# A three-block transformer layer on one core: statistics placed later, a split first unit, and a last product with tokens as rows

## The reference, cut to what matters

```python
x = x + 0.5 * swiglu_ffn(rmsnorm(x, ffn1_norm), ...)       # D_FF 2816
x = x + hybrid_mixer(rmsnorm(x, mix_norm), w_in, ...)      # sparse attention + gated linear attention
x = x + 0.5 * swiglu_ffn(rmsnorm(x, ffn2_norm), ...)
x = rmsnorm(x, final_norm)
# second layer
h = rms_norm(x, norm_pre_g);  proj = h @ w_in_2
y_a = pooled branch (window means, mix, silu(z_a));  y_b = mLSTM branch
merged = sigmoid(g_a + b0) * (y_a @ w_proj_pool) + sigmoid(g_b + b1) * (y_b @ w_proj_mlstm)
out = merged @ w_out_2
return x + rms_norm(out, norm_post_g)
```

## Time and profile before

| | us |
|---|---|
| median of 3 runs | 1795.54 |
| lowest, highest | 1794.02, 1796.08 |
| the profiled execution's own time | 1797.42 |
| its span, first to last instruction | 1795.6 |
| PE busy | 1693.2 (94% of the span) |
| PEld, weight loads beside matmuls | 1384.5 (77%) |
| DVE busy | 700.0 (39%) |
| ACT busy | 623.7 (35%) |
| POOL busy | 656.1 (37%) |

### The profile page before, as it was taken

One profiled execution on the slowest core, in us unless ns is written; L12 is line 12 of the kernel. 1 busy time (PEld: TensorE's weight loads), 2 busy tenths in 40 slices (PEclk: granted clock), 3 DMA queues, 4 the chain that ended last, 5 costly groups with the idle time before them and its releaser, 6 DMA issues.

```text
span 1795.6 us, 22547 instructions
## 1 busy us (share of the span) xinstructions
PE 1693.2 (94%) x7996; PEld 1384.5 (77%) x7996; DVE 700.0 (39%) x1157; ACT 623.7 (35%) x917; POOL 656.1 (37%) x281
## 2 busy tenths in 40 slices
PE   6999999999999999999999988889898999999997
PEld 5888888778886678888888877677677778877876
DVE  4333330225326744333330127473736331463223
ACT  4332231234236653223321234334343423234431
POOL 2444444433330024444444434222222223444443
PEclk9999999999999999999999989899999999999998
DMA  3322232233220002222222222121111112322221
GB/s 145 103 95 93 94 103 95 94 140 94 82 82 25 2 33 85 94 97 101 93 93 96 103 71 71 59 71 59 58 58 58 58 59 82 117 93 88 100 94 70
DMA packets 41663, 148.68 MB, mean 83 GB/s; under 512 B 4624, under 2 KB 4752, under 8 KB 41360
## 3 DMA queue, kind: packets, MB, share of 16 engines
q1 hardware_dynamic: 40112, 142.36, 23.4%
q10 hardware_dynamic: 1504, 5.66, 1.0%
HBM read 144.86 MB, written 2.10 MB: 82 GB/s over the span
## 4 chain that ended last, share of the span: by engine, by line
PE 47%; issue 39%; POOL 9%; DVE 3%; ACT 1%; POOLq 0%; DVEq 0%; ACTq 0%
PE ps L486 10%; PE ps L488 10%; PE ps L487 10%; POOL w_lo L432 9%; PE ps L566 3%; PE ps L568 3%; PE ps L567 3%; PE ps L724 1%; PE ps L494 1%; PE ps L736 1%; PE ps L746 1%; PE ps L501 1%; DVE scr L1518 1%; PE ps L647 0%; DVE scr L2068 0%
## 5 line engine op out<-in xcount | busy, mean ns | idle before, releaser
L432 POOL TENSOR_TENSOR w_lo<-w_raw,w_hi 128x1024 fp32r<-128x1024 f32 x262 | 636.1, 2428 | 1001.9 <-ACT w_hi L1067 992.4
L486 PE MATMUL ps<-h_hi,w_hi 128*128 128x512 f32 x1504 | 600.6, 399 | 25.7 <-POOL w_lo L432 20.7
L1067 ACT ACTIVATE w_hi<-w_raw 128x1024 fp32r<-128x1024 f32 x260 | 275.5, 1060 | 945.5 <-PE ps L488 763.5
L487 PE MATMUL ps<-h_lo,w_hi 128*128 128x512 f32 x1504 | 592.0, 394 | 0.0
L488 PE MATMUL ps<-h_hi,w_lo 128*128 128x512 f32 x1504 | 591.6, 393 | 0.0
L486 PEld LDWEIGHTS ps<-h_hi,w_hi 128*128 128x128 f32 x1504 | 287.2, 191 | 90.8 <-issue 22.1
L488 PEld LDWEIGHTS ps<-h_hi,w_lo 128*128 128x128 f32 x1504 | 286.3, 190 | 61.1
L487 PEld LDWEIGHTS ps<-h_lo,w_hi 128*128 128x128 f32 x1504 | 286.8, 191 | 58.9
L566 PE MATMUL ps<-hid_hi,w_hi 128*128 (+1 forms) x352 | 137.2, 390 | 1.8 <-POOL w_lo L432 1.8
L567 PE MATMUL ps<-hid_lo,w_hi 128*128 (+1 forms) x352 | 136.9, 389 | 0.0
L568 PE MATMUL ps<-hid_hi,w_lo 128*128 (+1 forms) x352 | 136.9, 389 | 0.0
(11 more groups left out here) (291 smaller groups left out, 1653.0 us busy)
## 6 DMA issues: line engine op xcount, KB each, us to landing
w_raw<-in_units SPq DMA_DIRECT2D x262, 512.0 KB, 3.2
x<-in_x SPq DMA_DIRECT2D x4, 512.0 KB, 7.1
w<-in_w ACTq DMA_DIRECT2D x1, 2048.0 KB, 8.1
out<-x SPq DMA_DIRECT2D x8, 256.0 KB, 2.0
scr<-proj ACTq DMA_DIRECT2D x8, 128.0 KB, 2.4
inv_count<-in_inv_count ACTq DMA_DIRECT2D x1, 1024.0 KB, 5.1
const<-in_const SPq DMA_DIRECT2D x1, 770.0 KB, 10.3
q_sc<-in_row_const ACTq DMA_DIRECT2D x1, 512.0 KB, 3.6
```

The costliest lines, as they stand in the source:

```text
L432: nc.gpsimd.tensor_tensor(w_lo[:, slot, :], w_raw[:, slot, :], w_hi[:, slot, :].bitcast(F32), ALU.subtract).then_inc(w_lo_done, 1)
L486: nc.tensor.matmul(ps[:, bank, :], whi, hi[:, k, :], start=(n == 0), stop=False)
L487: nc.tensor.matmul(ps[:, bank, :], whi, lo[:, k, :], start=False, stop=False)
L1067: nc.scalar.activation(w_hi[:, slot, :], w_raw[:, slot, :], ACT.Copy).then_inc(w_hi_done, 1)
```

## The change

1. **Later statistics.** Column sums stand behind the second unit, the spreading behind the third, in all three places. On ACT the heads and roots are put in the matching order; in `project` the copies that follow (`duplicate`) come one unit later.
2. **First unit split.** `first_unit` issues the two products with `w_hi` for all eight chunks and the eight with `w_lo` last, so `w_lo` is waited for after sixteen matmuls.
3. **Smaller first loads.** ACT first loads 8 columns of `param`, and the rest of `param` and `const` between the first heads. A one-element copy makes ACT load its table early. DVE starts when the gain is in.
4. **End of the first half of a feed-forward block.** DVE makes its four additions to `x` first, then four `raw_tail`; ACT converts the next unit's weights before the squares.
5. **x turned round.** In the pooled branch PE transposes `x` chunk by chunk (32 transposes in eight groups of four), ACT copies each group back. ACT also loads `g_row`, the last gain as a row on every partition (512 KB).
6. **Last product with tokens as rows.** Tokens of `m_hi` and `m_lo` are the stationary side, 512 columns of weights the moving one, with the eight chunks of `merged` as the outer loop and all eight banks filled at once. Per group of 128 tokens: ACT squares two banks with the sum accumulated, and takes the root; DVE the reciprocal, then two multiplications; POOL adds to six pieces, DVE to two; SP stores pieces of 128 tokens x 512 features. The 20 sums and 4 spreads at the end are gone.

```diff
-POOL_ADDS = 5
+POOL_ADDS = 6
...
+        PIECES = [(tt, half) for tt in range(TT) for half in range(2)]
+
+        def x_piece(n):
+            tt, half = PIECES[n]
+            return x[:, 4 * half:4 * half + 4, tt * P:(tt + 1) * P]
+
+        def sum_piece(n):
+            return scr[:, n, :].rearrange("p (c t) -> p c t", c=4)
...
+            for n, (tt, half) in enumerate(PIECES):
+                if n < POOL_ADDS:
+                    sp.wait_ge(x_out_pool, n + 1)
                 else:
-                    sp.wait_ge(x_out, c - POOL_ADDS + 1)
-                sp.dma_start(out[c * P:(c + 1) * P, :], x[:, c, :]).then_inc(out_sem, 16)
-            sp.wait_ge(out_sem, 16 * DC)
+                    sp.wait_ge(x_out, n - POOL_ADDS + 1)
+                sp.dma_start(out[tt * P:(tt + 1) * P, half * T:(half + 1) * T], scr[:, n, :]).then_inc(out_sem, 16)
...
+            for n in range(POOL_ADDS):
+                pool.wait_ge(sum_done, n + 1)
+                nc.gpsimd.tensor_tensor(sum_piece(n), sum_piece(n), x_piece(n), ALU.add).then_inc(x_out_pool, 1)
...
+            def first_unit(bank, chunks):
+                pe.wait_ge(w_hi_done, 1)
+                for k in range(DC):
+                    pe.wait_ge(*chunks(k))
+                    whi = w_hi[:, 0, k * P:(k + 1) * P]
+                    nc.tensor.matmul(ps[:, bank, :], whi, h_hi[:, k, :], start=(k == 0), stop=False)
+                    nc.tensor.matmul(ps[:, bank, :], whi, h_lo[:, k, :], start=False, stop=False)
+                pe.wait_ge(w_lo_done, 1)
+                for k in range(DC):
+                    mm = nc.tensor.matmul(ps[:, bank, :], w_lo[:, 0, k * P:(k + 1) * P], h_hi[:, k, :], start=False,
+                                          stop=(k == DC - 1))
                 mm.then_inc(unit_done, 1)
...
+                            opening = first and f == m == 0
+                            if opening and norm_of == 0:
+                                first_unit(4, raw(0))
+                            else:
+                                tile_unit(unit(u0 + 2 * f + m, 4, i), 4 + 2 * f + m, h_hi, h_lo,
+                                          raw(norm_of) if opening else None)
+                            if first and (f, m) == (0, 1):
+                                column_sums(norm_of)
+                            elif first and (f, m) == (1, 0):
+                                row_of_roots(norm_of)
...
                     tile_unit(unit(U_PROJ + u), project_bank(u), h_hi, h_lo, raw(1) if u == 0 else None)
-                    if u == 0:
+                    if u == 1:
                         column_sums(1)
-                    elif u == 1:
+                    elif u == 2:
                         row_of_roots(1)
...
-                with pe.Fori(0, DC) as i:
+                for j in range(DC):
+                    pe.wait_ge(ev_done, EV_POOL + j + 1)
+                    tile_unit(unit(U_POOL + j), 2 + j % 2, h_hi, h_lo)
+                    if j == 1:
+                        pe.wait_ge(mg_done, DC + 2)
+                    if j >= 4:
+                        pe.wait_ge(xt_done, j - 3)
+                    for tt in range(TT):
+                        mm = nc.tensor.transpose(ps[:, 4 + j % 4, tt * P:(tt + 1) * P], x[:, j, tt * P:(tt + 1) * P], ident)
+                    mm.then_inc(xt_ready, 1)
+                with pe.Fori(DC // 2, DC) as i:
                     for j in range(2):
                         pe.wait_ge(ev_done, EV_POOL + 2 * i + j + 1)
                         tile_unit(unit(U_POOL + j, 2, i), 2 + j, h_hi, h_lo)
+                pe.wait_ge(xt_done, DC)
...
-                pe.wait_ge(mg_done, 2 * DC + 2)
-                def two(i, chunks=None):
-                    for j in range(2):
-                        pe.wait_ge(out_done, 2 * i + j + 1)
-                        tile_unit(unit(U_OUT + j, 2, i), 2 + j, m_hi, m_lo, chunks if j == 0 else None)
-
-                two(0, lambda k: (m_lo_done, k + 1))
-                with pe.Fori(1, DC // 2) as i:
-                    two(i)
-                norm(5, "first")
-
-            pe.wait_ge(param_in, 16)
-            pe.wait_ge(small_in, 16)
+                for k in range(DC):
+                    u, _, slot = unit(U_OUT + k)
+                    pe.wait_ge(w_lo_done, u + 1)
+                    pe.wait_ge(m_lo_done, k + 1)
+                    for tt in range(TT):
+                        if k == 0 and tt >= 2:
+                            pe.wait_ge(mg_done, 2 * DC + tt - 1)
+                        tok = slice(tt * P, (tt + 1) * P)
+                        for half in range(2):
+                            acc, at = ps[:, 2 * tt + half, :], slice(half * T, (half + 1) * T)
+                            nc.tensor.matmul(acc, m_hi[:, k, tok], w_hi[:, slot, at], start=(k == 0), stop=False)
+                            nc.tensor.matmul(acc, m_lo[:, k, tok], w_hi[:, slot, at], start=False, stop=False)
+                            mm = nc.tensor.matmul(acc, m_hi[:, k, tok], w_lo[:, slot, at], start=False, stop=(k == DC - 1))
+                        if k == DC - 1:
+                            mm.then_inc(out_done, 1)
+                    if k < DC - 1:
+                        mm.then_inc(unit_done, 1)
...
                     for f in range(2):
-                        head(unit(u0 + 2 * f + 2, 4, i))
+                        if not (first and f):
+                            head(unit(u0 + 2 * f + 2, 4, i))
                         if first and f == 0:
+                            head(unit(u0 + 3))
                             root(norm_of)
+                            head(unit(u0 + 4))
                             root_row(norm_of)
-                            head(unit(u0 + 2 * f + 3, 4, i))
                         act.wait_ge(scaled_done, FT * n + 2 * i + f + 1)
...
                 streams(0, 4)
+                head(unit(ud + kps + 2))
                 squares(norm_of + 1, 0, 4)
-                head(unit(ud + kps + 2))
...
                     head(unit(U_PROJ + u + 2))
-                    if u == 0:
+                    if u == 1:
                         root(1)
-                    elif u == 1:
+                    elif u == 2:
                         root_row(1)
...
+                    act.wait_ge(xt_ready, j + 1)
+                    nc.scalar.activation(x[:, j, :], ps[:, 4 + j % 4, :], ACT.Copy).then_inc(xt_done, 1)
...
+                        act.dma_start(g_row[:, :], dram["g_post_row"]).then_inc(g_row_in, 16)
...
+                for i in range(DC - 2):
+                    head(unit(U_OUT + i + 2))
+                load_root()
+                for tt in range(TT):
+                    act.wait_ge(out_done, tt + 1)
+                    nc.scalar.activation(merged[:, 2 * (tt % 2):2 * (tt % 2) + 2, :], ps[:, 2 * tt:2 * tt + 2, :], ACT.Square,
+                                         accum_out=g_col[:, tt:tt + 1]).then_inc(osq_done, 1)
+                    act.wait_ge(osq_done, tt + 1)
+                    nc.scalar.activation(r_col[:, tt:tt + 1], g_col[:, tt:tt + 1], ACT.Sqrt, scale=1.0 / D, bias=c_("eps")
+                                         ).then_inc(orms_done, 1)
...
-            act.dma_start(param[:, :], dram["param"]).then_inc(param_in, 16)
-            act.dma_start(const[:, 0:FIRST_CONST], dram["const"][:, 0:FIRST_CONST]).then_inc(small_in, 16)
-            act.wait_ge(param_in, 16)
+            act.dma_start(param[:, 0:DC], dram["param"][:, 0:DC]).then_inc(gain_in, 16)
+            act.wait_ge(spare_done, 1)
+            nc.scalar.activation(spare[:, :], spare[:, :], ACT.Copy)
+            act.wait_ge(gain_in, 16)
...
+                    if c == 2:
+                        act.dma_start(const[:, 0:FIRST_CONST], dram["const"][:, 0:FIRST_CONST]).then_inc(small_in, 16)
+                    else:
+                        act.dma_start(param[:, DC:], dram["param"][:, DC:]).then_inc(param_in, 16)
...
-                        if gain is not None and d % 4:
+                        if gain is not None and d > 4:
                             raw_tail(next_norm, d - 1, gain)
                     if gain is not None:
-                        raw_tail(next_norm, 4 * half + 3, gain)
+                        for c in range(0 if half == 0 else DC - 1, 4 * half + 4):
+                            raw_tail(next_norm, c, gain)
...
+                dve.wait_ge(g_row_in, 16)
+                dve.wait_ge(xt_done, DC)
+                for n, (tt, half) in enumerate(PIECES):
+                    if half == 0:
+                        dve.wait_ge(orms_done, tt + 1)
+                        chain.link(nc.vector.reciprocal(r_col[:, tt:tt + 1], r_col[:, tt:tt + 1]))
+                    nc.vector.scalar_tensor_tensor(scr[:, n, :], ps[:, n, :], r_col[:, tt:tt + 1], g_row[:, half * T:(half + 1) * T],
                                                    ALU.mult, ALU.mult).then_inc(sum_done, 1)
-                for c in range(POOL_ADDS, DC):
-                    add(c)
-
```

(10 more changed lines are left out.)

59 lines of the change are left out of this document (21 added, 38 removed).

## The result

The changed kernel takes 1778.34 us (median of 4 runs, 1777.70 to 1782.81) beside 1795.17 us of the kernel before: a ratio of 0.991 (0.9895 to 0.9929), some 17 us less. Forecast were 1770.3 and a range of 1765.5 to 1776.5. The time lies 1.8 us above the range and 8.0 us above the forecast.

The account below looks back on a forecast made before the run. PE was taken as the bound, busy 94% of the span, limited by its 128 x 512 matmuls. Terms -8.0 - 1.8 - 5.9 - 2.3 + 3.0 - 1.7 - 8.5 = -25.2 from 1795.54 gave 1770.3, range 1765.5 to 1776.5.

Parts of the forecast that it names:

- Opening: Kernel start: PE starts earlier and sums no longer hold it; fourth unit starts at 31.8 instead of 39.8, 8.0 us earlier.
- the first rival: At the kernel's start `h_lo` stays the bound, PE runs longer at the lower clock: 5.2 instead of 8.0, 1773; chance 0.17.
- First block's middle: First feed-forward block, at 335.69: PE's wait for a `w_lo` goes, as ACT's squares now stand behind its `w_hi`: -1.8 us.
- projections: Column sums before the projections' spreading: the wait and slow clock behind it go, covered by the second unit: -5.9 us.
- Second feed-forward block: Column sums of the second feed-forward block: the wait goes as in the projections, less a new `w_lo` wait: -2.3 us.
- the small wait that was to appear under the old one: Second feed-forward block: the second unit's `w_lo` is ready only at 700.50, 0.6 us behind.
- Pooled branch: Eight groups of four transposes add 4.0 us on PE, a `w_lo` wait of 1.04 goes: +3.0 us net.
- Last product: Start of the last product: PE's wait of 1.71 us goes, since each `m_lo` chunk is needed only by its unit: -1.7 us.
- Tail: After the last matmul: the span ends 10.6 us later instead of 19.1, -8.5 us (7 to 10).
- the stages that the change leaves alone: Unedited stages: their waits and lower-clock stretches need not come out alike when everything shifts, 2 us either way.
- The lower clock that I had as a rival: Pooled branch: the clock falls behind each of eight transpose groups, nine matmuls at 0.43: +15 us, 1785; chance 0.03.
- Slower weight loads: Last product: activations loaded anew per matmul no longer run beside the matmuls: 36.7 us added, 1807; chance 0.02.

Follow-up runs that it names:

- early transposes: Changed kernel with the transposes of x moved from pooled branch to waits in the mLSTM's first head: 1776.2 us; with 64 small matmuls also split, 1771.3 us.

## Why the prediction was wrong, point by point

- **Opening: right, slightly too high.** TensorE starts at 7.13 and reaches the fourth unit at 32.42 (forecast 31.8, before 39.8): 7.4 instead of 8.0. Timelines of TensorE and VectorE in the changed kernel:

```profile
14.19 0.79 PE L509 MATMUL ps<-h_hi,w_hi 128*128 128x512 f32 x1 [1.18 <-DVE h_lo L1577]
...
16.92 2.99 PE L513 MATMUL ps<-h_hi,w_lo 128*128 128x512 f32 x8
...
25.22 0.95 PE L520 MATMUL ps<-const,scr 128*128 128x1 f32 x8
...
31.61 1.05 PE L527 MATMUL ps<-const,r_col 128*128 128x128 f32 x8
```

```profile
8.07 7.39 DVE L1577 SCALAR_TENSOR_TENSOR h_lo<-x,param,h_hi 128x512 fp32r<-128x512 f32 x6 [1.08 <-ACT h_hi L1137]
```

  `h_lo` ends at 15.46, near what was put (15.8), and stays the bound, as the first rival had it: VectorE needs 7.39 us for six instructions that take some 0.7 each when undisturbed. The eight products with `w_lo` took 2.99 us, so most ran at the slow pace, and the first unit ends at 19.75, not 19.2. The sums and the spreading wait for nothing.
- **First block's middle and projections: right.** With the opening 15.63 against 15.7; by the same matmuls in both traces 7.4 is the opening, 2.1 the middle (forecast 1.8) and 6.1 the projections (5.9). The wait of 1.83 us at 335 and that of 4.28 us in front of the sums have no counterpart in the changed kernel.
- **Second feed-forward block: right.** By the same matmuls ahead of and in the block 2.1, against 2.3. The 2.81 are of a window that also holds the norms, and that window takes 513.5 to 515.9 us in the traces of kernels that do the same work in it; the small wait that was to appear under the old one is there:

```profile
693.20 0.50 PE L499 MATMUL ps<-h_hi,w_hi 128*128 128x512 f32 x1 [0.63 <-POOL w_lo L445]
```

- **Pooled branch: right.** 2.51 against 3.0. Timeline of TensorE at one of the eight groups and at the mix:

```profile
1550.73 0.60 PE L1045 MATMUL ps<-const,x 128*128 128x128 f32 x4
...
1626.42 0.51 PE L1065 MATMUL ps<-y_hi,w_hi 128*128 128x512 f32 x1 [1.84 <-issue]
```

  The next unit starts 0.35 us behind a group's start, and its second matmul 0.32 us behind that, where 0.23 is usual: 0.44 us a group, 3.5 for the eight, less the wait of 1.04 us that is gone. The branch's clock stays at 1.00 in the window above. The rule of the Trainium skill ("TensorE: Matmul & The Clock Gate", Part 4: PE-mode transpose) that transposes do not count as activity cost nothing here: between units of matmuls, four transposes brought no stretch at 1.2 GHz in any of the eight places. Moving them shows 2.4 us net, with the wait of 1.02 us back.
- **Last product: the wait of 1.71 us is gone, the gain is 0.43.** Behind the wait of 1.84 us at 1626.42, which had been 1.74 before, the clock now falls to 0.50 for 3.4 us. That takes 1.6 us. The term itself was right: in the kernels with early transposes, which lack this stretch, the stage takes 142.5 us, 2.0 less than before.
- **Tail: right.** 10.35 against 10.6. Timelines of ScalarE, VectorE, GpSimd and the SyncE queue:

```profile
1770.74 1.02 ACT L1516 ACTIVATE merged<-ps 128x1024 f32<-128x1024 f32 x1
1771.67 0.19 ACT L1516 ACTIVATION_READ_ACCUMULATOR merged<-ps 128x1 f32 x1
...
1774.31 3.36 DVE L2149 TENSOR_TENSOR scr<-scr,x 128x512 f32<-128x512 f32 x2
...
1769.27 7.86 POOL L485 TENSOR_TENSOR scr<-scr,x 128x512 f32<-128x512 f32 x6 [5.81 <-DVE scr L2145]
...
1770.59 7.87 SPq L435 DMA_DIRECT2D out<-scr  x8
```

- **The step that failed** is the sentence on the stages that the change leaves alone: "2 us either way, about one such stretch as it was priced above". In the profiles they cost 8.28 + 2.14 = 10.4 us, and 1.3 more at the mix. By the medians the shortfall is 8.0 us; no trace of a median run says how it divides. The attention stage alone has taken values between 222.5 and 230.8 us in the study, of the same work. The trace of before had its three stretches there, of 13.6 us together, and two places where the loss would come (64 matmuls of 31 columns; the mixed small work at the attention's start) were to be seen in it. I took their clock as a property of the stage and gave its change the size of one stretch. The traces show that it is not fixed to the stage's work, and that several stretches move together. The change's own terms without the last product were forecast at 23.5 and measured 15.63 + 2.81 - 2.51 + 8.76 = 24.7, or 24.0 with 2.1 for the second block.
- **The rivals.** None came true with its price. The first was right that `h_lo` still bounds the opening and that TensorE runs slowly for longer, but this cost 0.6 us and not 2.8. The lower clock that I had as a rival was put behind the transposes; it came elsewhere. Slower weight loads were not to be seen: the last product's matmuls end at the usual distance of 0.23 us.
- **The base.** 1795.54 was the median of three runs; in the later sets the kernel before had medians of 1798.6, 1795.4 and 1797.4. As a ratio the forecast is 1770.3 / 1795.54 = 0.986. That is outside the interval of the first comparison (0.9895 to 0.9929) and at or just below the lower edge of the two later ones (0.9860 to 0.9934, 0.9862 to 0.9910).

What stays open is what sets the stretches. The same instructions take 415.53 and 416.01 us against 414.62 before any edit acts, the same program has mLSTM stages 3.3 us apart, and most of the kernels that ran more than once have runs 5 to 10 us apart. So something outside the program's instructions takes part, and no run here varied it on purpose. How much of the shortfall the change brings by moving the program, and how much the execution, the runs do not separate. Whether the burst itself must bring a stretch was not settled either.

## What to carry to other kernels

Price an edit by what it does, and separately allow for what its shift does to every later stage whose TensorE work is thin (small matmuls, short waits): here up to 8 us in one stage of 225, more than most of the edits. To tell such a loss from an effect of the edit, compare equal stretches of both traces by busy time and granted clock, then shift the kernel by a microsecond of harmless work and see whether the loss stays. See also which of its runs a trace shows: a trace of the slowest run explains the slowest run. And keep the kernel under study in every set, beside its variants. Work that only has to be done some time, like the transposes, belongs in a wait that exists already.

## What was not expected of the hardware

- The same 64 matmuls take from 4.39 us to 5.71 us, and the 24-matmul unit behind them runs at 1.2 GHz or not, and their distance from the program's start does not tell which: at full clock when reached at 459.81, not when reached at 459.63 or at 460.01.
- 0.9 us of added TensorE work changed which times come: eight of twelve runs of the kernel before with it are slower than all 17 without it. The changed kernel with it had a median 3 us lower than in its first four runs, but those are of another set, and the intervals of the two ratios overlap.
- At the start the windows show a granted clock of 1.00 while matmuls of 512 columns still follow each other at 0.43 us: before from 11.50 to about 16.3, after from 7.13 to about 19, longer by its waits between chunks. The window of the changed kernel:

```profile
7.00:13.00 6.00, 4.96 (x10) 2.94 (x10) 4.93 (x4) 5.04 (x9) 4.29 (x2) 1.00 1.05 403
```
